# A decoder step's expert stage: token rows in a ring of four buffers, expert weights in three pairs of buffers to the end

## The reference

```
g_sel = argmax(x @ w_group + b_group)                 # 1 of 4 groups
top_i = top_k(expert logits inside the group + b, 2)  # 2 of its 8 experts
gate  = g_prob[g_sel] * softmax(the two logits)
for e in range(32):
    gu = x @ w_gate_up[e]                             # 1024 -> 2 x 256
    h  = silu(gu[:, :256]) * gu[:, 256:]
    y += gate[:, e] * (h @ w_down[e])                 # 256 -> 1024
out = layernorm(ALPHA * x + y)
```

## Time and profile before

| | |
|---|---|
| median of 3 runs | 604.76 us (601.89 to 605.17) |
| profiled execution | 602.56 us, span 600.9 us |
| TensorE busy | 518.8 us, 86% of the span |
| VectorE busy | 373.2 us, 62% |
| ScalarE busy | 191.4 us, 32% |
| GpSimd busy | 134.0 us, 22% |
| moved by DMA | 157.95 MB, mean 263 GB/s |

### The profile page before, as it was taken

How to read it: one execution, slowest core, us unless ns; L and a number is a source line. 1 busy time by engine, 2 the same in 40 slices (tenths; PEclk the granted TensorE clock), 3 DMA queues, 4 the chain that set the end, 5 groups by cost and what they waited for, 6 DMA issues and landing times.

```text
span 600.9 us, 8960 instructions
## 1 busy us (share of the span) xinstructions
PE 518.8 (86%) x3296; PEld 281.0 (47%) x3296; DVE 373.2 (62%) x722; ACT 191.4 (32%) x356; POOL 134.0 (22%) x156
## 2 busy tenths in 40 slices
PE   5999999999979879899999898888887777767761
PEld 4887788874355443445556743333332222222220
DVE  1642059898933576652258666677886477666686
ACT  0100374214243644121142122444444244432340
POOL 1001054500025760000000201233323222221231
PEclk9999999999979999999999899999999899999997
DMA  9940008570606932001978599999999999999951
GB/s 302 405 155 6 1 1 331 213 269 1 279 5 230 395 116 87 2 1 59 417 290 342 180 420 406 409 396 419 415 415 411 419 418 419 415 415 418 401 193 43
DMA packets 34010, 157.95 MB, mean 263 GB/s; under 512 B 12680, under 2 KB 12680, under 8 KB 20016
## 3 DMA queue, kind: packets, MB, share of 16 engines
q1 hardware_dynamic: 20592, 127.46, 52.9%
q0 software_dynamic: 10752, 29.59, 13.0%
q10 hardware_dynamic: 2624, 0.34, 0.4%
HBM read 160.12 MB, written 21.23 MB: 302 GB/s over the span
## 4 chain that ended last, share of the span: by engine, by line
PE 56%; DMA 26%; DVE 8%; ACT 7%; issue 3%; SPq 0%; POOL 0%; DVEq 0%; POOLq 0%; ACTq 0%
DMA arena_o<-in_w_gu 19%; PE ps L489 17%; PE ps L748 8%; PE ps L962 8%; PE ps L985 4%; PE ps L651 3%; PE ps L589 2%; PE ps L635 2%; DVE arena_s L1477 2%; PE ps L672 2%; DMA first_rows<-arena_s,known 1%; DMA x_rows<-arena_s 1%; PE ps L555 1%; DMA known<-slot_table 1%; DMA slot_table<-arena_s 1%
## 5 line engine op out<-in xcount | busy, mean ns | idle before, releaser
L962 PE MATMUL ps<-arena_w,arena_s 128*64 128x512 f32 x368 | 109.2, 605 | 24.1 <-DMA arena_w<-in_w_gu 12.3
L489 PE MATMUL ps<-arena_w 128*128 128x260 f32 x416 | 94.5, 388 | 6.7 <-DMA arena_w<-in_w_in 6.2
L489 PEld LDWEIGHTS ps<-arena_w 128*128 128x128 f32 x416 | 79.7, 193 | 21.0 <-DMA arena_w<-in_w_in 6.2
L962 PEld LDWEIGHTS ps<-arena_w,arena_s 128*64 128x64 f32 x368 | 33.2, 139 | 96.9 <-issue 66.4
L985 PE MATMUL ps<-arena_w,cs 128*64 128x512 f32 x184 | 56.1, 615 | 20.8 <-ACT cs L1260 20.8
L748 PE MATMUL ps<-arena_o,arena_s 128*128 128x512 f32 x128 | 58.3, 601 | 1.6 <-DVE arena_s L1601 1.6
L962 PE MATMUL ps<-arena_o,arena_s 128*64 128x512 f32 x112 | 50.2, 595 | 0.0
L1477 DVE STREAM_TRANSPOSE arena_s<-arena_w 128x1024 f32<-128x1024 f32 x36 | 41.8, 1214 | 8.3 <-PE ps L589 8.2
L2150 POOL DMA_INDIRECT first_rows<-arena_s,known x15 | 18.0, 1202 | 113.9 <-ACT arena_s L1267 105.1
L1910 DVE TENSOR_TENSOR arena_s<-arena_s,ps 128x256 f32<-128x256 f32 x16 | 6.7, 421 | 56.5 <-ACT arena_s L1256 56.5
L985 PEld LDWEIGHTS ps<-arena_w,cs 128*64 128x64 f32 x184 | 16.0, 141 | 51.0 <-issue 30.3
(11 more groups left out here) (349 smaller groups left out, 897.3 us busy)
## 6 DMA issues: line engine op xcount, KB each, us to landing
arena_w<-in_w_gu SPq DMA_DIRECT2D x46, 1024.0 KB, 19.9
arena_w<-in_w_dn SPq DMA_DIRECT2D x23, 1024.0 KB, 19.9
arena_o<-in_w_gu SPq DMA_DIRECT2D x14, 1024.0 KB, 23.2
arena_o<-in_w_dn SPq DMA_DIRECT2D x7, 1024.0 KB, 23.8
arena_w<-in_w_in SPq DMA_DIRECT2D x13, 512.0 KB, 14.1
arena_o<-in_w_out SPq DMA_DIRECT2D x1, 4096.0 KB, 13.5
arena_s<-in_w_gu SPq DMA_DIRECT2D x4, 1024.0 KB, 8.1
arena_w<-in_xT SPq DMA_DIRECT2D x4, 520.0 KB, 6.7
```

The source lines that it names most:

```text
L489: last = mm(ps[rows, b + n, 0:HALF], lhs(k), rhs(k)[:, n * HALF:(n + 1) * HALF], start=(k == 0), stop=(k == ks - 1))
L962: last = mm(ps[64 * e:64 * e + 64, 2 + q, :], xgT[:, k, CAP * e:CAP * (e + 1)], gu_w[2 * slots + e][:, k, :], start=(k == 0), stop=(k == K ...
```

## The change

- The row buffers are a ring of four (`ring(n)` is `n % 4`), at the first four places of before. The gather for pair n+2 is now issued first in GpSimd's `pair_step(n)`, two pairs ahead, and waits until the output of pair n-2, which lay in the same buffer, has landed.
- That leaves the third pair of weight buffers free: the buffers go 0, 1, 2, 0, 1, 0, 1, 2 in a round of eight pairs, and `refill` follows them.
- `finish`, `root` and `scatter_out` are one pair behind in place of two. `gather_other(n+1)` is issued at the end of `pair_step(n)`. The buffers for it are two, also for the last pair.
- In the last pair the other expert's rows are added first and the pair's own output last, straight from PSUM; and pair 14 is finished on VectorE ahead of `hidden(15)`.
- Behind the last products TensorE runs five small matmuls whose results nobody reads.
- GpSimd keeps the bound of its indirect transfers in a register, and computes the counts for the last waits ahead of time.

```diff
+BUFFER = (0, 1, 2, 0, 1, 0, 1, 2)
...
-S_XG = [5120, 6144, 0, D, S_RT] + [S_SLOT + D * n for n in range(3)]
-S_YO = [S_SLOT + 3 * D, 2 * D, S_SLOT + 4 * D]
+S_XG = [5120, 6144, 0, D]
+S_YO = [S_RT, 2 * D]
...
+def pair_buffer(n):
+
+    return n if n < HEAD else BUFFER[(n - HEAD) % BODY]
+
+
+def before_in(n):
+
+    d = 1
+    while BUFFER[(n - HEAD - d) % BODY] != pair_buffer(n):
+        d += 1
+    return d
+
+
+def weights_landed(it, n):
+
+    if n < HEAD:
+        return 32
+    m, q = n - HEAD, pair_buffer(n)
+    per = BUFFER.count(q)
+    v = 32 * (2 + m // BODY * per + BUFFER[:m % BODY].count(q))
+    return it[0] * (4 * per) + v if isinstance(it, tuple) else it * (32 * per) + v
...
         def ring(n):
 
-            return n % BODY
-
-        def other(it, n):
-
-            return 2 if isinstance(it, tuple) and n == NPAIR - 1 else n % 2
+            return n % 4
...
-            def refill(q, e, used):
-
+            def refill(it, n):
+
+                q, used = pair_buffer(n), nth(it, n, add=1 - before_in(n))
+                e = 2 * n if it is None or isinstance(it, tuple) else (it * (2 * BODY) + 2 * n) % NE
                 for half, done in enumerate((gu_half, gu_ps)):
                     sp.wait_ge(done, used)
-                    for n in range(2):
-                        gate_up(2 * q + n, slice(e + n, e + n + 1) if isinstance(e, int) else bass.ds(e + n, 1), half)
+                    for j in range(2):
+                        gate_up(2 * q + j, slice(e + j, e + j + 1) if isinstance(e, int) else bass.ds(e + j, 1), half)
                 sp.wait_ge(dn_ps, used)
-                for n in range(2):
-                    down(2 * q + n, slice(e + n, e + n + 1) if isinstance(e, int) else bass.ds(e + n, 1))
-            refill(0, 6, 1)
-            refill(1, 8, 2)
+                for j in range(2):
+                    down(2 * q + j, slice(e + j, e + j + 1) if isinstance(e, int) else bass.ds(e + j, 1))
+            refill(None, HEAD)
+            refill(None, HEAD + 1)
             sp.wait_ge(routed, 1)
             n_rounds = sp.value_load(rounds[0:1, 0:1], min_val=1, max_val=MAXR)
             past = sp.value_load(rounds[0:1, 1:2], min_val=0, max_val=(MAXR - 1) * NPAIR)
-            with sp.Fori(0, n_rounds * (NE // 4) - 3) as it:
-                refill(0, (it * 4 + 10) % NE, it * 2 + 4)
-                refill(1, (it * 4 + 12) % NE, it * 2 + 5)
-            refill(0, NE - 2, past + (NPAIR - 2))
+            with sp.Fori(0, n_rounds * 2 - 1) as it:
+                for n in range(HEAD + 2, HEAD + 2 + BODY):
+                    refill(it, n)
+            for n in range(HEAD + 2 + BODY, NPAIR):
+                refill((past,), n)
...
-                q, slots = n % 2, n if n < HEAD else (n - HEAD) % 2
-                landed_count = 32 if n < HEAD else nth(it, n - HEAD, 2, 32, 64) if not isinstance(it, tuple) else \
-                    it[0] * 16 + ((n - HEAD) // 2 * 32 + 64)
+                q, slots, landed_count = n % 2, pair_buffer(n), weights_landed(it, n)
...
                 if not last_pair:
                     turn_tokens(it, n + 1)
+                else:
+                    for _ in range(5):
+                        mm(ps[:, 7, 0:P], ident[:, :], ident[:, :], start=True, stop=True)
...
-                if n >= 2:
-                    root(None, n - 2)
+                if n >= 1:
+                    root(None, n - 1)
...
                 hidden((past,), n)
                 own_out((past,), n)
-                root((past,), n - 2)
+                root((past,), n - 1)
...
-            root((past,), NPAIR - 3)
+            root((past,), NPAIR - 2)
             hidden((past,), NPAIR - 1, True)
-            root((past,), NPAIR - 2)
             root((past,), NPAIR - 1)
...
-            def own_part(it, n, last_pair=False):
+            def own_part(it, n):
 
                 x, g = xg[ring(n)], known[:, n // QUAD % 2, 2, n % QUAD:n % QUAD + 1]
                 dve.wait_ge(known_landed, nth(it, n, QUAD, 16, 16))
                 dve.wait_ge(residual_step, nth(it, n, 1, 2, 2))
+                dve.wait_ge(ya_done, nth(it, n, add=1))
+                stt(x, yb[n % 2], g, x, ALU.mult, ALU.add).then_inc(own_added, 1)
+
+            def finish(it, n, last_pair=False):
+
+                x = xg[ring(n)]
                 if last_pair:
-                    dve.wait_ge(dn_ps, nth(it, n, add=1))
-                    y = ps[:, 5:7, :]
-                    x = x.rearrange("p (a b) -> p a b", a=2)
+                    dve.wait_ge(residual_step, nth(it, n, 1, 2, 2))
                 else:
-                    dve.wait_ge(ya_done, nth(it, n, add=1))
-                    y = yb[n % 2]
-                stt(x, y, g, x, ALU.mult, ALU.add).then_inc(own_added, 1)
-
-            def finish(it, n):
-
-                x = xg[ring(n)]
-                dve.wait_ge(own_added, nth(it, n, add=1))
+                    dve.wait_ge(own_added, nth(it, n, add=1))
                 if n > 0:
-                    dve.wait_ge(yo_landed[other(it, n)], 16 if other(it, n) == 2 else nth(it, n + 1, 2, 16))
-                    stt(x, yo[other(it, n)], known[:, n // QUAD % 2, 3, n % QUAD:n % QUAD + 1], x, ALU.mult, ALU.add).then_inc(finish_step, 1)
+                    dve.wait_ge(yo_landed[n % 2], nth(it, n + 1, 2, 16))
+                    stt(x, yo[n % 2], known[:, n // QUAD % 2, 3, n % QUAD:n % QUAD + 1], x, ALU.mult, ALU.add).then_inc(finish_step, 1)
                     dve.wait_ge(finish_step, nth(it, n, 1, 4, 1))
                     dve.wait_ge(mean_done, nth(it, n))
+                if last_pair:
+                    halves = x.rearrange("p (a b) -> p a b", a=2)
+                    dve.wait_ge(dn_ps, nth(it, n, add=1))
+                    stt(halves, ps[:, 5:7, :], known[:, n // QUAD % 2, 2, n % QUAD:n % QUAD + 1], halves, ALU.mult, ALU.add).then_inc(own_added, 1)
+                    dve.wait_ge(own_added, nth(it, n, add=1))
                 first = V.bn_stats(bn[:, 0, :], x[:, 0:512])
...
-                if n >= 2:
-                    finish(it, n - 2)
+                if n >= 1:
+                    finish(it, n - 1)
                 own_part(it, n)
...
-            finish((past,), NPAIR - 3)
+            finish((past,), NPAIR - 2)
             hidden((past,), NPAIR - 1)
-            finish((past,), NPAIR - 2)
-            own_part((past,), NPAIR - 1, True)
-            finish((past,), NPAIR - 1)
+            finish((past,), NPAIR - 1, True)
...
+            limit = ctx.enter_context(pool.register("limit"))
+            pool.reg_mov(limit, TOK - 1)
+
             def gather_rows(n, at):
 
                 G.indirect_dma_start(out=xg[ring(n)], out_offset=None, in_=x1_rows,
                                      in_offset=bass.IndirectOffsetOnAxis(ap=at, axis=0),
-                                     bounds_check=TOK - 1, oob_is_err=False).then_inc(gathered[n % 4], 16)
+                                     bounds_check=limit, oob_is_err=False).then_inc(gathered[n % 4], 16)
...
-                G.indirect_dma_start(out=yo[other(it, n)], out_offset=None, in_=first_rows,
+                G.indirect_dma_start(out=yo[n % 2], out_offset=None, in_=first_rows,
                                      in_offset=bass.IndirectOffsetOnAxis(ap=place(1, n), axis=0),
-                                     bounds_check=TOK - 1, oob_is_err=False).then_inc(yo_landed[other(it, n)], 16)
-
-            def scatter_out(it, n):
-                ready, = number(nth(it, n, add=1))
+                                     bounds_check=limit, oob_is_err=False).then_inc(yo_landed[n % 2], 16)
+
+            def scatter_out(it, n, ready=None, before=None):
+                if ready is None:
+                    ready, before = number(nth(it, n, add=1), nth(it, n, 1, 16))
                 fixed()
+                if n > 0:
+                    pool.wait_ge(out_landed, before)
                 pool.wait_ge(out_ready, ready)
                 G.indirect_dma_start(out=y_out, out_offset=bass.IndirectOffsetOnAxis(ap=place(1, n), axis=0),
-                                     in_=xg[ring(n)], in_offset=None, bounds_check=TOK - 1,
+                                     in_=xg[ring(n)], in_offset=None, bounds_check=limit,
                                      oob_is_err=False).then_inc(out_landed, 16)
 
             def pair_step(it, n):
 
-                scatter_own(it, n)
-                if n >= 3:
-                    outs, = number(nth(it, n - 2, 1, 16))
-                    fixed()
-                    pool.wait_ge(out_landed, outs)
-                if n >= 2:
-                    scatter_out(it, n - 2)
-                if n >= 1:
-                    gather_other(it, n)
-                if n == 1:
-                    pool.wait_ge(dn_ps, HEAD)
-                if n < HEAD:
-                    gather_rows(n + 4, first_at[:, n + 4:n + 5])
-                elif not isinstance(it, tuple) or n + 4 < NPAIR:
```

(24 more changed lines are left out.)

5 lines of the change are left out of this document (2 added, 3 removed).

## The result

The changed kernel takes 623.1 us (median, which is also the profiled execution; span 621.5) against 604.96 for the kernel before on the same chip (profiled 602.56). One of its four executions took 1093.8 us and is left out of the median and the ratio, as is one of 633.2 us among the four of `e3_warm`. The forecast was 608.4 with a range to 617. The direction was right, and so was the start of the mechanism; the loop was priced wrong, and the forecast loss of 3.6 us was a fifth of what came.

What follows compares the result with a forecast made beforehand. TensorE's pace (13.4 us a pair) was taken as the bound first, weights over DMA (16.7) from pair 8. Statistics 5.2 us later, last-pair gain included, less 1.5: +3.7 on 602.56, plus 2.2 to the median: 608.4, range 599.5 to 617.

Steps and rivals of the forecast that it cites:

- the loop: Ring of four, pairs after 4: queued row transfers make 15.2 us a pair, against TensorE's 13.4 and the weights' 16.7.
- the correction for the dry stretch: Near 447 us the weight queue may run dry, row transfers land faster: 0 to 3 us back, 1.5 taken.
- Part 1: Third pair of weight buffers: weights asked for a pair earlier, but no idle DMA engine to fill, so gain 0.
- The start: Rows 4 wait for output 0 to land; ScalarE's copy of pair 3's output starts at 412.4, 13.3 us late.
- A(4): Start of ScalarE's copy of pair 4's output: 427.6, 15.1 us late, as rows 5 land at 420.7.
- The price of a transfer: Row transfers on GpSimd's queue: 8.3 us alone, 3.0 us behind the one ahead when queued.
- Faster than the weights' 16.7: From pair 8 on weights are slower than the ring's 15.2, so a delay of some 20 us is partly eaten up.
- Part 3: Finish one pair behind on VectorE: 0 from pair 1 to 14, as long as the other's rows are there.
- The clock: TensorE's granted clock at the last pair: held, L985 ends at 587.3 and 2.9 us are gained; fallen, 588.6 and 2.2.
- Part 4: Last pair's new order: statistics start 17.7 us after ScalarE's copy of pair 14's output, 2.9 us less.
- Rival 3: SyncE's wait ahead of pair 8's weights is met too late, DMA loses time: 611.5 to 618 us, chance 0.18.
- The upper end: Gaps of 3.7 us between queued row transfers: 16.6 us a pair, +17.0, shortened by a dry weight queue, some 618.

Runs made afterwards that it cites:

- e3_warm: Changed kernel with small 128x128 constant matmuls on TensorE ahead of pair 3's turned rows (36) and each later odd pair's (10): 1.0277 of the kernel before.
- second series: The changed kernel, unedited, run again against the kernel before: ratio 1.0355.
- e1: Changed kernel with weight pairs alternating between two buffers instead of three: 1.0295 of the kernel before.
- e8_ring8: Changed kernel with the ring of eight row buffers and two pairs of weight buffers of before, finish still one pair behind: 1.0014 of the kernel before.
- e6: Changed kernel with finished rows written to the other's-rows buffer and pair 1's gather of the other's rows issued a step later: 1.0076 of the kernel before.
- e7: The changed kernel with both row-queue edits of e6, and two weight buffers instead of three: 1.0087 of the kernel before.
- e2: Changed kernel with its three weight buffers used strictly in turn: 1.0361 of the kernel before.

## Why the prediction was wrong in size

The forecast had the last statistics 3.7 us later than before, the profiled execution has them 20.6 us later. Of the 16.9 us between the two, the loop is 11.1, the start of this execution, which is not the change, 3.7, the correction for the dry stretch 1.5, the end 1.3; A(2) to A(4) was 0.7 us less than forecast.

- **Part 1, third buffer, 0: right**, by `e1` and `e7`. The argument (no idle DMA engine to fill) fits, but no run has a third buffer where weights alone set the pace, so it stays an argument.
- **The start, A(3) 13.3 us late: right for the profile shown** (+14.4; +17.9 in the second series). Its chain is the one in the timeline above.
- **A(4) 15.1 us late: nearly** (+14.4). That rows 5 would cost another 1.8 us was too much; the second pair of each lap follows at TensorE's own 13.4.
- **The loop: this is the step that failed.** I wrote "That is 3.0 + 0.9 + 8.3 + 3.0 = 15.2 us a pair: slower than TensorE's 13.4, faster than the weights' 16.7", and from it A(4) to A(14) in 152.0 us, 7 less than before. It took 163.1. The sum followed GpSimd's queue through one step. The ring's chain runs through five engines and queues and over two pairs: rows, TensorE's turn, VectorE's `finish`, the output, and its landing. With my prices and the trace before (turned rows to `finish` 4.8 us, 392.22 to 397.03; `finish` to the finished output 6.1, 410.52 to 416.64) it would have been 8.3 + 4.8 + 6.1 + 0.9 + 8.0 + 0.9, 29.0 us for two pairs, no better a figure; the measured 31.9 has rows at 9.2 (their median landing from 453 us on), outputs at 8.6 to 11.6 up to the gather that waits for them, and in every other lap 1.3 us for the clock. Five laps at 31.9 instead of 30.4 are 7.5 us of the 11.1; the other 3.6 lie at the last lap's end, with a landing of 10.4 and down products of 6.6 us.
- **The price of a transfer.** The medians of the earlier trace rows were of a kernel in which rows were asked for four pairs ahead and never waited for. Reading 8.3 as "alone" was too low: in the ring rows took 8.0 to 10.4 us from 453 us on, 9.2 in the middle. The correction of 1.5 us for faster transfers in the dry stretch came true as a landing (rows 7, asked for at 444.94, took 3.5 us) and not as a gain: TensorE turned them at 454.98, straight behind its own products, and that lap, to 477.40, was 32.5 us long.
- **"Faster than the weights' 16.7", so that the delay is eaten up.** The kernel before needs 15.9 a pair from A(4) to A(14), as its first three run at 13.4. A ring of 15.2 would have returned 7 us of the debt; one of 16 returns nothing.
- **Part 3 at nothing: wrong at one place.** "As long as the other's rows are there" was the condition, and for pair 1 it fails: 5.9 us in `e8_ring8`. In the changed kernel this lies beside the wait for rows 4, which is longer; it comes out when that wait is repaired (in `e6` TensorE turns rows 4 at 392.56 without a wait, VectorE waits 8.49 us for the other's rows, TensorE 6.03 us for VectorE's hidden values, and A(2) to A(3) is 21.5 us against 13.6).
- **The clock, priced at the end alone.** In the loop it was put at nothing. Down products behind a wait take 5.0 to 6.6 us instead of 3.65. On the path it is about 3 us by the reading above.
- **Part 4, 2.9 us: right**, A(14) + 17.7 in `e8_ring8`. The changed kernel got 1.6 of it, since its last down products ran at the low clock in spite of the five filler matmuls (5.4 us; 3.65 in `e8_ring8` with the same five). The filler took 1.4 us and not 0.7, at ten records for five matmuls.
- **Rival 3**, a dry weight queue, occurred as described; `e2` shows that it cost nothing. Its price of 611.5 to 618 was nearer to the truth than the forecast, by luck: it had another reason.
- **The upper end, a slip in the sum.** With gaps of 3.7 us I had A(14) near 594, and wrote +17.0. From 593.6 the statistics start at 611.3, which is +19.2, and the time would be 602.56 + 19.2 + 2.2, some 624. Less what a dry weight queue was to shorten, for which there was no figure, that was written as some 618 and as a range to 617. The measured 623.1 lies under the corrected end, but with gaps and a loop that were not those of the sum, so this is no merit of it.

## What to carry to other kernels

A buffer ring that is made shorter turns work that was ahead of time into a closed loop. Follow that loop once round through every engine and both its transfers, count how many pairs one lap serves, and compare the lap with the slowest pace over the whole stretch, not with that of its slow half. Price its transfers as they are beside the bulk stream, with a margin: outputs and rows priced here at 8.0 and 8.3 us took 8.6 to 11.6 and 8.0 to 10.4 in the loop. And a condition such as "as long as the rows are there" is to be checked at the first step, where nothing has run ahead yet.
